# Key pages on partition quarters: a new layout for the paged keys of a decode attention kernel

## What is computed

```python
def diff_attend(q, q_pos, k, v, k_pos, lam):
    s = jnp.einsum('bqhcd,bkhcd->bhcqk', q, k).astype(jnp.float32) * (QK_HEAD ** -0.5)
    mask = k_pos[None, :] <= q_pos[:, None]
    s = jnp.where(mask, s, -jnp.inf)
    p = jax.nn.softmax(s, axis=-1)
    a = p[:, :, 0] - lam * p[:, :, 1]
    return jnp.einsum('bhqk,bkhd->bqhd', a, v.astype(jnp.float32))

k_past = cache_k[l, page_table].reshape(bs, past, N_HEADS, 2, QK_HEAD)
v_past = cache_v[l, page_table].reshape(bs, past, N_HEADS, V_HEAD)
```

## Time and profile before

| what | before |
|---|---|
| median of the runs | 2381.55 us (2377.91 to 2386.35, 3 runs) |
| span of the profiled execution | 2380.2 us |
| PE busy, share of the span | 1984.2 us, 83% |
| DVE busy | 1056.3 us, 44% |
| ACT busy | 486.3 us, 20% |
| POOL busy | 354.0 us, 15% |
| bytes that the DMA engines moved | 404.21 MB, mean 170 GB/s |

### The profile page before, as it was taken

How to read it: one execution, slowest core, us unless ns; L and a number is a source line. 1 busy time by engine, 2 the same in 40 slices (tenths; PEclk the granted TensorE clock), 3 DMA queues, 4 the chain that set the end, 5 groups by cost and what they waited for, 6 DMA issues and landing times.

```text
span 2380.2 us, 47877 instructions
## 1 busy us (share of the span) xinstructions
PE 1984.2 (83%) x17492; PEld 1635.0 (69%) x17492; DVE 1056.3 (44%) x1528; ACT 486.3 (20%) x831; POOL 354.0 (15%) x544
## 2 busy tenths in 40 slices
PE   4699999668786876878785794999999997999992
PEld 1277898557665765767674793777777776888881
DVE  2424211666675665766561557111111112455457
ACT  0300111021212112121221203111211111333331
POOL 0000000223242423324232104200000000000003
PEclk7799999799897988889796896999999998999996
DMA  9711223779897979879896410121212123411112
GB/s 302 256 36 35 72 71 118 250 245 341 285 385 282 385 279 346 314 283 381 298 354 234 156 35 18 54 71 53 88 53 70 53 88 128 137 41 37 36 32 91
DMA packets 210968, 404.21 MB, mean 170 GB/s; under 512 B 24426, under 2 KB 88938, under 8 KB 210788
## 3 DMA queue, kind: packets, MB, share of 16 engines
q1 hardware_dynamic: 161012, 261.51, 31.9%
q0 software_dynamic: 41488, 136.35, 15.5%
q10 hardware_dynamic: 8320, 4.19, 0.6%
HBM read 377.53 MB, written 24.51 MB: 169 GB/s over the span
## 4 chain that ended last, share of the span: by engine, by line
PE 65%; DVE 13%; SPq 7%; DMA 7%; issue 6%; ACT 1%; DVEq 0%; ACTq 0%
PE psum L753 26%; PE psum L1002 11%; PE psum L761 10%; PE psum L852 5%; DVE k_turned L1432 4%; SPq L445 4%; SPq L449 3%; DMA ada_w<-w_ada 3%; DMA k_ring<-cache_k 3%; PE psum L1009 2%; PE psum L862 2%; DVE p_t L424 2%; PE psum L736 2%; PE psum L832 1%; DVE x_lo L1282 1%
## 5 line engine op out<-in xcount | busy, mean ns | idle before, releaser
L852 PE MATMUL psum<-k_turned,q_blocks 128*32 128x128 f32 x4096 | 332.3, 286 | 85.6 <-DVE k_turned L1432 84.9
L852 PEld LDWEIGHTS psum<-k_turned,q_blocks 128*32 128x32 f32 x4096 | 291.7, 114 | 137.1 <-issue 98.5
L1432 DVE STREAM_TRANSPOSE k_turned<-k_ring 128x2048 f32<-128x2048 f32 x128 | 295.4, 2308 | 6.6 <-DMA k_ring<-cache_k 5.7
L753 PE MATMUL psum<-x_hi,w_hi 128*128 128x512 f32 x896 | 281.3, 395 | 0.0
L753 PE MATMUL psum<-x_lo,w_hi 128*128 128x512 f32 x896 | 277.3, 391 | 0.0
L753 PE MATMUL psum<-x_hi,w_lo 128*128 128x512 f32 x896 | 276.0, 389 | 0.0
L1301 DVE TENSOR_TENSOR w_lo<-w_raw,w_hi 128x2048 fp32r<-128x2048 f32 x37 | 86.9, 2350 | 363.1 <-ACT w_hi L1057 353.5
L1002 PE MATMUL psum<-d_hi,h_hi 128*128 128x256 f32 x704 | 209.2, 297 | 12.2 <-DVE d_lo L1646 11.1
L862 PE MATMUL psum<-v_ring,p_t 128*32 128x128 f32 x4096 | 191.7, 295 | 19.3 <-DMA v_ring<-cache_v 18.9
L1002 PE MATMUL psum<-d_lo,h_hi 128*128 128x256 f32 x704 | 199.9, 284 | 0.0
L1002 PE MATMUL psum<-d_hi,h_lo 128*128 128x256 f32 x704 | 199.7, 284 | 0.0
(11 more groups left out here) (228 smaller groups left out, 2525.1 us busy)
## 6 DMA issues: line engine op xcount, KB each, us to landing
k_ring<-cache_k SPq DMA_DIRECT2D x256, 256.0 KB, 8.0
k_ring<-cache_k POOLq DMA_DIRECT2D x256, 256.0 KB, 6.1
v_ring<-cache_v SPq DMA_DIRECT2D x256, 256.0 KB, 8.8
v_ring<-cache_v POOLq DMA_DIRECT2D x256, 256.0 KB, 6.0
ada_w<-w_ada SPq DMA_DIRECT2D x12, 2048.0 KB, 9.6
w_raw<-w_in SPq DMA_DIRECT2D x12, 1024.0 KB, 5.3
w_raw<-w_gate SPq DMA_DIRECT2D x11, 1024.0 KB, 5.4
w_raw<-w_up SPq DMA_DIRECT2D x11, 1024.0 KB, 6.3
```

Of the source, the lines that this page charges most:

```text
L753: last = mm(psum[:, 2 * ft + c, 0:CH], w[:, s, k, ft * P:(ft + 1) * P], x[:, k, c * CH:(c + 1) * CH], start=k == 0 and j == 0, stop=k == K ...
L852: last = mm(psum[QUAD * h:QUAD * (h + 1), g % 2, 0:GP * QUAD], q_blocks[:, h, d, :], k_turned[:, g % 2, :, h * HD + d * QUAD:h * HD + (d + ...
L1432: v.transpose(k_turned[:, g % 2].rearrange("p j n -> p (j n)"), k_ring[:, g].rearrange("p j n -> p (j n)")).then_inc(k_free, 1)
```

## The change

The key ring gets another layout, and three things follow from it.

1. **Loads.** Key page j of a group goes to partitions 32j to 32j+31 alone. Each of these partitions gets four rows of the page, one from each quarter, one behind the other: 8 KB a partition, in four pieces of 2 KB. Value pages are loaded as before. The bytes, the number of DMAs, their order and their semaphores stay.
2. **Weights.** After DVE's block transpose, which is the same instruction, partition group j holds page j, and the columns run over (quarter, position). The block diagonal of `q_blocks` now separates pages in place of quarters, and `q_blocks` is the same data. After the softmax's transposes the partitions are (quarter, position) already, as the value products need them. `regroup` goes; `keep_weights` copies one PSUM bank, 128 x 512, in one instruction: 4 copies in place of 16, two on ACT and two on DVE. `p_t` has the same size with its columns in another order, and `value_group` takes its weights from the new place.
3. **Key products.** In `key_group` the loop over the dim pieces is now outside the loop over the heads, so that products which follow each other go to different 32-partition groups of PSUM.

```diff
--- before.py
+++ after.py
@@ -250,7 +250,7 @@
         ar = Area(y_conv_at)
         k_rows = ar("k_rows", [P, NT, HD])
         q_rows = ar("q_rows", [P, NT, HD])
-        p_t = ar("p_t", [P, z.PAGES, QUAD])
+        p_t = ar("p_t", [P, REVS * RING, P])
         max_row = place("max_row", [1, 2, P], F32, lam_rows_at)
 
 
@@ -414,15 +414,10 @@
 
             return link, loop
 
-        def regroup(copy, j):
-
-
-            got = psum[QUAD * j:QUAD * (j + 1), 0:REVS, :].rearrange("p r n -> p (r n)").rearrange(
-                "p (g h a q) -> p g h a q", h=H, a=4, q=8)
-            to = p_t[:].rearrange("p (g j) (h q) -> p g j h q", j=4, q=8)
-            for a in range(4):
-                last = copy(to[QUAD * a:QUAD * (a + 1), :, j], got[:, :, :, a, :])
-            return last
+        def keep_weights(copy, r):
+
+            return copy(p_t[:, r * RING:(r + 1) * RING].rearrange("p g (a h q) -> p g a h q", a=4, q=8),
+                        psum[:, r, :].rearrange("p (g h a q) -> p g a h q", h=H, a=4, q=8))
 
         def rope(x1_, x2_, cos, sin, tmp, link, done):
 
@@ -446,8 +441,12 @@
                                           min_val=0, max_val=z.POOL - 1)
                     if j == 0:
                         eng.wait_ge(free, (b * REVS + r) * RING + g + 1)
-                    eng.dma_start(ring[:, g, j, :], pages[ds(page, 1)].rearrange("o p d -> p (o d)")
-                                  ).then_inc(landed[g], 16)
+                    if ring is k_ring:
+                        eng.dma_start(ring[QUAD * j:QUAD * (j + 1), g],
+                                      pages[ds(page, 1)].rearrange("o (a t) d -> t (o a) d", t=QUAD)).then_inc(landed[g], 16)
+                    else:
+                        eng.dma_start(ring[:, g, j, :], pages[ds(page, 1)].rearrange("o p d -> p (o d)")
+                                      ).then_inc(landed[g], 16)
 
             keys, values = (k_pages, k_ring, k_in, k_free), (v_pages, v_ring, v_in, v_free)
             with eng.Fori(0, REVS) as r:
@@ -847,8 +846,8 @@
                 n = (b * REVS + r) * RING + g
                 pe.wait_ge(k_free, RING + 1 + n)
                 pe.wait_ge(s_bank_free, n + 1)
-                for h in range(H):
-                    for d in range(4):
+                for d in range(4):
+                    for h in range(H):
                         last = mm(psum[QUAD * h:QUAD * (h + 1), g % 2, 0:GP * QUAD], q_blocks[:, h, d, :],
                                   k_turned[:, g % 2, :, h * HD + d * QUAD:h * HD + (d + 1) * QUAD],
                                   start=d == 0, stop=d == 3)
@@ -859,7 +858,7 @@
                 pe.wait_ge(v_in[g], (b * REVS + r + 1) * (16 * GP))
                 for j in range(GP):
                     for h in range(H):
-                        last = mm(psum[QUAD * h:QUAD * (h + 1), 2, 0:P], p_t[:, (r * RING + g) * GP + j, :],
+                        last = mm(psum[QUAD * h:QUAD * (h + 1), 2, 0:P], p_t[:, r * RING + g, j * QUAD:(j + 1) * QUAD],
                                   v_ring[:, g, j, h * HD:(h + 1) * HD], start=False, stop=stop and j == GP - 1)
                 last.then_inc(v_free, 1)
 
@@ -1109,8 +1108,8 @@
                     part = s_rows[:, r * BANK:(r + 1) * BANK] if r < REVS else s_rows[:, NEW0:SC]
                     go(part, part, ACT.Exp, bias=dec[:, 1:2], accum_out=dec[:, 2 + r:3 + r]).then_inc(exp_done, 1)
                 act.wait_ge(p_turned, b + 1)
-                for j in range(0, 2):
-                    last = regroup(copy, j)
+                for r in range(0, 2):
+                    last = keep_weights(copy, r)
                 last.then_inc(p_by_act, 1)
 
             def keep_output(b):
@@ -1451,8 +1450,8 @@
                 if h is not None:
                     head_start(h)
                 dve.wait_ge(p_turned, b + 1)
-                for j in range(2, 4):
-                    regroup(v.tensor_copy, j)
+                for r in range(2, REVS):
+                    keep_weights(v.tensor_copy, r)
                 v.tensor_copy(p_new[0:QUAD, :].rearrange("p (h q) -> p h q", q=8),
                               psum[0:QUAD, MISC, P:2 * P].rearrange("p (h a q) -> p h a q", a=4, q=8)[:, :, 0, :]).then_inc(p_by_dve, 1)
                 link(v.tensor_reduce(dec[:, 12:13], psum[:, MISC, 384:384 + REVS + 1], AX_X, ALU.add))
```

## The result

The changed kernel takes **2638.34 us** (median of 4 runs, 2634.42 to 2645.47) against 2382.48 us of the kernel before beside it: a ratio of 1.1071, 95% interval 1.1052 to 1.1091. The forecast was 2437 us and the range ended at 2550. The sign was right, the size was not: the loss is 256 us where 55 were forecast, and it is larger than that of rival B (2570 us).

What follows compares the result with a forecast made beforehand. Transfers nearly fill a step: 89.8 us stream plus 16.2 us gap. At x = 1.4 seven steps give +54, step 0 +5, the end -4: +55 on 2381.55 us, forecast 2437 us, range 2330 to 2550.

Steps and rivals of the forecast that it cites:

- rival B: Attention-stage loads: every key page moves at half rate, x = 1.96, +188 us, 2570 us; chance 0.13.
- chain at the softmax: From a step's last keys to the next step's first key transpose: 4.2 + 1.1 = 5.3 us a step shorter.
- rival A: Attention-stage loads: the transfers lose nothing, x = 1, -41 us, 2340 us; chance 0.27.
- The two weights' copies: DVE after the softmax: two 128x512 copies take 1.4 us instead of 5.63, 4.2 us less a step.
- the key products: PE, per key group: 1.1 us instead of 2.13 with heads inside; 1.1 us a step, about 190 us busy.
- The signs named for a loss: Attention-stage windows: share 1.0 at clearly under 385 GB/s, and DVE idle before key transposes because of k_ring, previously 6.6 us.
- x: Attention-stage loads: a key page's time relative to before; taken as 1.4, bounds 1 and 1.96, break-even 1.16.
- the stream: Transfer part of a step, 89.8 us at 386 GB/s; claimed to grow by 43.5(x-1).
- the ada_bias row: Trace row of a lone load onto 32 partitions: 197 GB/s against 386, taken as the bound x = 1.96.
- the gap: Rest of a step around the softmax, 16.2 us; shrinks by 5.3 from the chain and 10.9(x-1) from slower slot filling.
- no 5 us at 0: Sign in the attention stage's windows: transfers no longer stop for 5 us, the softmax stall being mostly gone.
- Step 0: First attention step, keys only: loses 0 to 10 us from slower key loads, taken as +5.

Runs made afterwards that it cites:

- (d): Kernel that only loads pages, no computation: SP alone loads every page onto the one quarter of partitions 0 to 31; 208 GB/s.
- the fastest kernel: Kernel before, plus gathered keys, DVE's next queries and first key transpose ahead of its weights wait, POOL loading value groups 1 and 3: 2278.25 us, ratio 0.9543.

## Why the prediction was right and wrong

**Bound and chain: right.** Transfers bound the stage, and the chain at the softmax is worth 5.3 us a step: with the landing put back a step lost 5.2 us and the kernel 41, which is rival A's 41. The two weights' copies took 1.29 us where 1.4 was said, the key products 192.9 us where 190 was said. The signs named for a loss came: share 1.0 at far less than 385 GB/s, and DVE idle because of `k_ring`.

**The term that was mis-sized: x.** "I take 1.4, a bit nearer to the value rows" was the step that failed. Without the mean stall, the stream of a step went from 103.8 - 12.3 = 91.5 us to 140.4 - 5.6 = 134.8 (with the landing put back it is 98.6 - 7.0 = 91.6), so 43.5(x - 1) = 43.3 and **x = 2.0**. The rates of the windows shown, 378 and 247 GB/s, give 2 x 378/247 - 1 = 2.06. Nothing of what a key page leaves idle was filled. The reason given for less, that value pages use the other half, is half true. With free queues it happens: 291 GB/s with half of the bytes keys is x = 2 x 386/291 - 1 = 1.65. With the kernel's rings it is 2 x 386/259 - 1 = 1.98, and the trace shows the value pages waiting with the keys. So what the prediction left out is what the rings do to a mixture of keys and values; that they cost it is shown, by which wait is not.

That x came out at the bound from the ada_bias row, 1.96, is in part luck, and doesn't show rival B's reason, that every key page moves at half rate. One quarter alone moves 208 GB/s (d), which is 1.86, and keys on all four quarters move 247 from two free queues, which is 1.56.

**The second term: the gap.** At x = 1.96 the prediction let it shrink by 5.3 + 10.4 us, to nothing; "no 5 us at 0" was to be the sign. It went from 12.3 to 5.6 us in the mean, and the sign came: the transfers stand at 0 for 4 us on end at most, where before it was 4 to 11. DVE's timeline of the changed kernel shows the chain at the longest stall, and a line of PE's there shows what holds it up:

```profile
807.48 2.30 DVE L1431 STREAM_TRANSPOSE k_turned<-k_ring 128x2048 f32<-128x2048 f32 x1
819.21 0.30 DVE L1398 BATCH_NORM_STATS2 o_stats<-psum 128x128 f32 x1 [9.42 <-PE psum L831]
...
835.67 1.29 DVE L419 COPY p_t<-psum 128x512 f32<-128x512 f32 x2 [5.07 <-PE psum L883]
...
840.67 2.31 DVE L1431 STREAM_TRANSPOSE k_turned<-k_ring 128x2048 f32<-128x2048 f32 x1
```

```profile
810.76 1.93 PE L861 MATMUL psum<-v_ring,p_t 128*32 128x128 f32 x32 [3.54 <-DMA v_ring<-cache_v]
```

From the last key transpose of a step to the first of the next it is 33.2 us, before 745.23 - 713.39 = 31.8. The copies gave their 4.3 us. But the step's last value pages come late, and PE's products and the prompt's rows (L1398) stand behind them: these start 11.7 us after the last transpose, 7.9 before, and the idle time of DVE that follows, ahead of the softmax, is 2 us longer too. So a new wait ate the gain. And the slots were full 28 us after that transpose (835 - 807), where they were full after some 23 before (736 - 713): 5 us more, not 10.4. The mean of the seven softmaxes says nearly the same: from transpose to transpose it is 27.0 us, 28.0 before and 23.7 with the landing put back. So of the 6.7 us that the gap lost, the chain gave 0.9 and the slower filling 5.8.

Put together: a step had +43.3 for the stream and -6.7 for the gap, +36.6, where x = 1.4 gave +17.4 and -9.7, +7.7. The 29 us between them, 26 of them in the stream, make in seven steps the 201 us between forecast and result. Step 0 (+9.8 for +5) and the end (-5.3 for -4) were small and right in sign. Rival B nearly had the stream (131.6 us) and missed by the gap, which it let close.

## What to carry to other kernels

Which partitions a load lands on is part of its price, as much as its bytes. A layout that spreads a tile over the partitions in four loads of 32 is not the same as one load of 128; before giving a load fewer partitions, look for the one row of the trace that has it alone, and don't count on other transfers to fill what it leaves idle when they share its queues and rings: free queues filled a part here (291 GB/s), queues with rings did not (259, and 247 in the kernel). A good layout need not be given up for that: a gather put the same pages on the same partitions, with a page's rows in another order, and the kernel moved 372 GB/s. And when a busy queue is to be relieved, look at how long it needs to issue one transfer: 1.3 us a page bound the end of the stage, which only showed once the rest was gone.

## What was not expected of the hardware

- 32 partitions at a distance of 4 move 365 GB/s, 64 neighbouring ones from 0 and 64 in turn only 234.
- Two queues on opposite halves move 295 GB/s, on the same half 206; in the kernel with its rings the split brought no more than 244.
- The DMA engines' busy share does not tell these apart: it is 1.07 at 208 GB/s and 1.04 at 388.
- One gather of 1 MB takes POOL about 1 us to issue (989 ns in the fastest kernel), where four pages took it 4 x 1.2 us, the reading of their numbers included.
